# RWKV-7 delta rule on one core: u's products between y's products with the state, and the second half of the grams ahead of the rest of y

## What is computed

```
def step(S, inp):
    r_t, w_t, k_t, v_t, kk_t, b_t = inp
    sa = jnp.einsum('bhvk,bhk->bhv', S, kk_t)
    S = S * w_t[:, :, None, :] - sa[..., None] * b_t[:, :, None, :] + v_t[..., None] * k_t[:, :, None, :]
    return S, jnp.einsum('bhvk,bhk->bhv', S, r_t)
```

## Time and profile before

| | us |
|---|---|
| median of 3 runs | 1451.32 (1449.02 to 1452.41) |
| the profiled execution | 1445.32, of which the span is 1443.5 |
| PE busy | 1371.0 (95%) |
| PE weight loads | 1207.8 (84%) |
| DVE busy | 778.6 (54%) |
| ACT busy | 614.1 (43%) |
| POOL busy | 240.5 (17%) |

### The profile page before, as it was taken

How to read it: one execution, slowest core, us unless ns; L and a number is a source line. 1 busy time by engine, 2 the same in 40 slices (tenths; PEclk the granted TensorE clock), 3 DMA queues, 4 the chain that set the end, 5 groups by cost and what they waited for, 6 DMA issues and landing times. The chain is left out here.

```text
span 1443.5 us, 32955 instructions
## 1 busy us (share of the span) xinstructions
PE 1371.0 (95%) x13740; PEld 1207.8 (84%) x13740; DVE 778.6 (54%) x1588; ACT 614.1 (43%) x1230; POOL 240.5 (17%) x335
## 2 busy tenths in 40 slices
PE   7999999999999899999999899999999999998997
PEld 7989899887899788888888568899999997665885
DVE  6737344687750157788788543741111213875445
ACT  6725345777851123344334431531111133886224
POOL 0000000000000146677566400000001000213000
PEclk9999999999999979899899999999999999999999
DMA  5723323567778254556564363042324355230202
GB/s 211 222 67 70 98 78 104 142 169 214 220 202 227 64 101 104 116 125 148 133 135 105 96 240 133 1 175 85 90 90 110 90 145 189 87 118 23 89 30 94
DMA packets 265269, 178.43 MB, mean 124 GB/s; under 512 B 169599, under 2 KB 239167, under 8 KB 264207
## 3 DMA queue, kind: packets, MB, share of 16 engines
q1 hardware_dynamic: 233159, 161.37, 39.5%
q10 hardware_dynamic: 31968, 15.04, 3.6%
HBM read 116.21 MB, written 60.46 MB: 122 GB/s over the span
## 5 line engine op out<-in xcount | busy, mean ns | idle before, releaser
L369 PE MATMUL mix_acc<-mix_high,mix_w_high 128*128 128x364 f32 (+1 forms) x768 | 178.6, 341 | 12.4 <-ACT mix_high L435 10.0
L369 PE MATMUL mix_acc<-mix_low,mix_w_high 128*128 128x364 f32 (+1 forms) x768 | 172.2, 333 | 0.6 <-DVE mix_low L589 0.6
L369 PE MATMUL mix_acc<-mix_high,mix_w_low 128*128 128x364 f32 (+1 forms) x768 | 171.1, 332 | 0.0
L369 PEld LDWEIGHTS mix_acc<-mix_high,mix_w_high 128*128 128x128 f32 x768 | 130.4, 190 | 32.1 <-issue 28.4
L369 PEld LDWEIGHTS mix_acc<-mix_low,mix_w_high 128*128 128x128 f32 x768 | 133.4, 190 | 1.2 <-DVE mix_low L589 0.9
L369 PEld LDWEIGHTS mix_acc<-mix_high,mix_w_low 128*128 128x128 f32 x768 | 134.0, 190 | 0.0
L603 DVE TENSOR_TENSOR mix_w_low<-mix_wt,mix_w_high 128x1024 fp32r<-128x1024 f32 x32 | 39.2, 1224 | 127.6 <-ACT mix_w_high L441 127.3
L1612 PE MATMUL out_acc<-qkvg_room_r_high,qkvg_room_w_high 128*128 128x364 f32 (+1 forms) x320 | 105.8, 331 | 1.4 <-DVE qkvg_room_w_low L1964 1.4
L1612 PE MATMUL out_acc<-qkvg_room_r_low,qkvg_room_w_high 128*128 128x364 f32 (+1 forms) x320 | 105.1, 329 | 0.0
L1612 PE MATMUL out_acc<-qkvg_room_r_high,qkvg_room_w_low 128*128 128x364 f32 (+1 forms) x320 | 105.1, 328 | 0.0
L455 ACT ACTIVATE mix_out<-mix_acc 128x364 f32<-128x364 f32 (+1 forms) x96 | 38.3, 472 | 146.0 <-PE mix_acc L369 145.9
(11 more groups left out here) (282 smaller groups left out, 3130.3 us busy)
## 6 DMA issues: line engine op xcount, KB each, us to landing
mix_wt<-in_w_in SPq DMA_DIRECT2D x32, 512.0 KB, 4.6
qkvg_room_wt<-in_w_att SPq DMA_DIRECT2D x20, 512.0 KB, 3.7
delta_bk<-scr_bk SPq DMA_DIRECT2D x68, 128.0 KB, 3.4
delta_kr<-scr_kr SPq DMA_DIRECT2D x17, 512.0 KB, 6.6
scr_kr<-mix_outs SPq DMA_DIRECT2D x16, 512.0 KB, 4.0
scr_bk<-mix_outs SPq DMA_DIRECT2D x16, 512.0 KB, 4.7
early_xpad<-in_xpad SPq DMA_DIRECT2D x8, 548.5 KB, 8.7
scr_xg<-early_xs SPq DMA_DIRECT2D x8, 544.0 KB, 3.0
```

The lines of the kernel that those rows point to most:

```text
L369: mm = pe.matmul(acc[:, s, k, 0:width], w[:, s, d, :], r[:, d, n0:n0 + width], start=d == 0 and q == 0, stop=d == DT - 1 and q == 2)
```

## The change

`make_u` and `begin_y` become one function, `make_u_and_begin_y`. For each pair it issues u's two products with the result in the other half (`FLIPPED`), so in off-diagonal quarters, and then y's two products with the state, in diagonal ones. The wait for `normed` (the centring and scaling of the chunk before, which uses the bank `wide`) stands ahead of all of them now. `turn_y` comes after both, then `make_grams(front, 1)`, then `end_y`. ScalarE's copies of u read the other half (`src[FLIPPED[p]]`), and the one-piece copy of chunk 16 to `lower` becomes two copies of 64 partitions.

```
-                def make_u(c):
+                def make_u_and_begin_y(c):
+
                     if c < SAMPLE:
                         pe.wait_ge(grown_kept, 6 * c + 6)
                     else:
                         pe.wait_ge(solved_wide, c + 1)
                     pe.wait_ge(z_kept, c + 1)
+                    if c:
+                        pe.wait_ge(normed, NORM * c)
                     for pair in range(DT):
+                        columns = slice(64 * pair, 64 * pair + 64)
+                        for p, half in enumerate(HALVES):
+                            u = pe.matmul(chain_bank[FLIPPED[p], columns], inverse(c, 1)[half, pair, :], z[half, pair, :], start=True, stop=True)
+                        if pair == DT - 1:
+                            u.then_inc(u_made, 1)
                         for half in HALVES:
-                            mm = pe.matmul(chain_bank[half, 64 * pair:64 * pair + 64], inverse(c, 1)[half, pair, :], z[half, pair, :], start=True, stop=True)
-                    mm.then_inc(u_made, 1)
+                            if c < SAMPLE:
+                                y = pe.matmul(wide_bank[half, columns], kr[half, c % 4, 1, pair, :], state[half, c % 2, pair, :], start=pair == 0, stop=False, skip_group_check=True)
+                            else:
+                                y = pe.matmul(wide_bank[half, columns], own_turned[half, pair, 1, :], unit64[half, :], start=pair == 0, stop=False, skip_group_check=True)
+                    y.then_inc(y_begun, 1)
...
                     if live(behind):
-                        make_u(behind)
+                        make_u_and_begin_y(behind)
                     if live(i - 2):
                         turn_y(i - 2)
...
-                    if live(behind):
-                        begin_y(behind)
-                        end_y(behind)
                     if live(front):
                         make_grams(front, 1)
+                    if live(behind):
+                        end_y(behind)
...
                     for p, half in enumerate(HALVES):
-                        act.activation(uv[half, c % 3, :, p, :], src[half], ACT.Copy).then_inc(u_kept, 1)
+                        act.activation(uv[half, c % 3, :, p, :], src[FLIPPED[p]], ACT.Copy).then_inc(u_kept, 1)
                     if c == SAMPLE:
...
-                        act.activation(lower[:], src, ACT.Copy).then_inc(u_plain_kept, 1)
+                        for p, half in enumerate(HALVES):
+                            act.activation(lower[half], src[FLIPPED[p]], ACT.Copy).then_inc(u_plain_kept, 1)
```

More of the change, by code:

```diff
@@ L1206, in make_s @@
                     mm.then_inc(s_made, 1)
-                def begin_y(c):
-                    if c:
-                        pe.wait_ge(normed, NORM * c)
-                    for pair in range(DT):
-                        for half in HALVES:
-                            o = wide_bank[half, 64 * pair:64 * pair + 64]
-                            if c < SAMPLE:
-                                mm = pe.matmul(o, kr[half, c % 4, 1, pair, :], state[half, c % 2, pair, :], start=pair == 0, stop=False, skip_group_check=True)
-                            else:
-                                mm = pe.matmul(o, own_turned[half, pair, 1, :], unit64[half, :], start=pair == 0, stop=False, skip_group_check=True)
-                    mm.then_inc(y_begun, 1)
                 def end_y(c):
@@ L1416, in _ @@
                         for b in range(NB):
-                            act.wait_ge(u_plain_kept, 1)
+                            act.wait_ge(u_plain_kept, 2)
                             act.activation(u_own[:, b], lower[:], ACT.Copy, scale=seq_mask[:, b:b + 1]).then_inc(u_owned, 1)
```

## The result

The changed kernel takes 1429.68 us (median of 4 runs, 1422.90 to 1432.47) against 1450.17 of the kernel before, now the median of four runs too: 20.5 us less, ratio 0.9854 with the 95% interval 0.9812 to 0.9896. The profiled execution took 1431.17 with a span of 1429.4, so 14.1 less than the span before. I had forecast 13.4 less and 1438, with 1429 as the lower end. The 95% interval of the first set stands for 15 to 27 us less, that of the second for 12 to 25: the size is known to some 6 us either way.

A forecast was written before the change was run, and what follows sets the result against it. PE and DVE are nearly full, bound by a ring of waits on PE's second grams. 15 turns x 0.93 = 14.0 us less, 0.6 back: 1445.3 to 1431.9 profiled, plus 6.0 gives 1438, range 1429 to 1446.

The forecast's parts named there:

- the ring of waits: DVE's second masks, block sums, GpSimd's pick, PE's spread, DVE's solve columns, y's scaling; waits each turn for PE's second grams.
- the turn: A middle turn at full clock goes from 16.83 us to some 15.9, 0.93 less, in turns 1 to 15.
- The block in four quarters: On PE, u and the begun y as 64 records take 1.03 us instead of 2.38; upper bound 2.22.
- The new wait and the DVE idle: PE waits some 0.74 us before second grams; DVE's 0.95 before second masks goes; reciprocal waits about 0.45.
- the loss at the third level products: On PE, the third level products wait for the inverse ready at 760.30, which costs 0.06 us.
- Turn 17: At the end of u's chain, ScalarE's copy of the second half adds 0.6 us.
- I expect as many falls as before: The clock falls to half level as often as before, give or take one or two, 4.4 us a fall.
- PE idled before the spread: Before the clock falls at 599 and 705, PE ran narrow second-level products, then idled ahead of the spread.
- The 6.0 carried over from the profile to the median: The median without a profile lies 6.0 us above the profiled execution; added again for the changed kernel, giving 1437.9.
- Rival B: The quarters of u and y do not overlap: block 2.22 us, turn gains about 0.55, time 1444.6; chance 0.12.
- Rival D: Slower: PE's moved idle makes the clock fall in more turns, 4.4 us each, 1460 with five more; chance 0.09.

The follow-up runs named there:

- e3: Changed kernel with u's products in the diagonal quarters, shared with y, order and alternation kept: 1429.2 us against 1446.7 before, ratio 0.9898.
- f1: The changed kernel as it is, run again beside more runs of the kernel before: 1428.8 us against 1449.1, ratio 0.9871.
- e4: Changed kernel with one extra 256-column matmul per turn, result overwritten, in PE's gap before the spread: 1430.5 us against 1446.7 before, ratio 0.9885.
- e1: Kernel before with only the order changed, second half of the grams ahead of the end of y: 1425.2 us against 1446.7, ratio 0.9867.
- e2: Changed kernel with the second grams back behind the end of y, four quarters kept: 1450.1 us against 1446.7 before, ratio 1.0031.
- g1: e2 with one extra 256-column matmul per turn where PE waits for ScalarE's copies of u: 1462.9 us against 1446.5 before, ratio 1.0112.

## Why the prediction was right or wrong

The direction was right, and so was the ring of waits. The size was not: 20.5 against 13.4. Two terms failed: the turn, taken at 0.93 where 1.05 was measured, and the clock, whose part in the difference I put at nothing and in the level at a fixed 6.0. By the prediction's steps:

- **The block in four quarters: right.** 1.10 for the 1.03 taken; without the quarters 2.02 for the 2.22 (e3). By the Trainium skill's rule ("TensorE: Matmul & The Clock Gate", "The mechanism") that weight loads overlap only across row groups, the four quarters would have taken what the diagonal took. The traces disagree with it, 1.10 us in the changed kernel against 2.02 in e3.
- **The new wait and the DVE idle: right.** 0.70 for 0.74; the second masks' wait is gone; the reciprocal waits 0.52 for the 0.45 forecast.
- **The turn: too small, 0.93 for 1.05.** I took the idle of 0.95 as the gain. But a DVE instruction starts about 0.07 before the end printed for the one ahead of it (742.86 against 742.28 + 0.65), so from start to start the removed wait was worth 1.02: 753.45 - 751.85 = 1.60 before, 742.86 - 742.28 = 0.58 now. And I let the loss at the third level products stand (0.06), which did not come. 15 turns make 15.8 for 14.0: 1.8 us of the miss of 7.
- **Turn 17: right.** +0.6.
- **"I expect as many falls as before", and the clock left out of the difference: the larger part of the miss.** 15.8 less 0.6 makes 15.2. At 60 us of half clock the two lines lie 15 us apart, at 80 us 17 (16 to 18 by resampling the executions). So the layout of the turn accounts for the change at the same clock to within 2 us; this excess stays open. Most of the other 3 us of the 20.4 in f1's set is how long the clock happened to be down in the executions compared: 77 us for 84 in the kernel before, 2.5 us at 0.385 each. The first set can't be split that way, since of its kernel before only the profile has a clock on record.
- **The number of falls was right, their length not.** From the begun z of turn 1 to that of turn 15, 14 turns, the profile of the kernel before has 249.1 us, which is 13.3 more than 14 x 16.84. The two profiles of the changed kernel have 232.2 and 230.8, so 11.1 and 9.7 more than 14 x 15.79. Each has two falls after the stretch at 550. In the kernel before both last 10 us and cost 4.3 to 4.4 in their turn; in the changed kernel one lasts 10 us and costs 4.0 to 4.1, the other lasts 3.4 and costs 0.9. That is the 2 to 4 us, in three single profiles.
- **"PE idled before the spread" ahead of the falls at 599 and 705: wrong for the first.** PE had stopped 0.89 without a releaser ahead of the level products, and did not wait before the spread (the rows under e4).
- **The 6.0 carried over from the profile to the median: wrong.** It is no property of the kernel. The profiled execution of the kernel before, 1445.3 at a clock of 0.976, was one of its less disturbed; that of the changed kernel, 1431.2 at 0.971, lies 3.0 above the median of its three others. For the profiled execution I had 1431.9, and 1431.2 came: a hit that is partly luck, for its 14.1 are 16.0 gained from the first grams of turn 1 to those of turn 15 (248.78 and 232.78), 4.3 lost ahead of them, where the granted clock from 500 to 560 was 0.66 for 0.80, and 2.4 gained behind.
- **Rival B, too low in its price.** I had PE bind the turn at 0.55 gained if nothing overlaps. The most common turns gained 1.01 in e3 and 0.87 in e1, the mean ones 0.80 and 0.64. The step that failed is the block at its upper bound with a further idle for its start: the second grams start 3.69 after the first in e3 where I had 3.90, and the level products 0.4 earlier than before where I had 0.2, enough for the block sums to stay the latest in a turn in which PE does not stop.
- **Rival D was real, in another kernel.** e2 has the shorter turn and no gain, g1 is 16 us slower. In the changed kernel the gap before the spread got shorter instead (0.67 for 1.02).

What the title of the change names first, the overlap of u and y, is worth 0.04 of the 1.05 by e3's most common turn (the quarters alone) and 0.18 by e1's (with the alternation). By the means of the turns and at the same clock it is worth more, 4 to 7 us of the 17, which fits the slack that it leaves PE for its stops; in the median times nothing of this is seen, since e1 and e3 spent less time at half clock. Alone (e2), the quarters gained nothing in time. The order of the grams is the larger part by every measure.

## What to carry to other kernels

Look for the ring of waits across engines and move the producer that the ring waits for; here two lines of order did what the overlapped products could not, because their time came out of a wait. Where single executions scatter by a per cent, plot each one's time against its time at half clock: here that turned a scatter of 17 us from lowest to highest into one of 1.4 about a line, and told a change of the work from a change of the clock. Read all turns at full clock and not only the most common one, for a rare stop of an engine lengthens the turn only where that engine has no slack. A shorter turn can lose all its gain to the clock, as in e2, if it leaves PE idle beside sparse products.

## What was not expected of the hardware

- One matmul of 0.6 to 0.7 us per turn that computes nothing, in a gap of 1.0 to 1.2 behind narrow products, took 14 us off (1435.2 against 1449.1); from 560 to 790 the granted clock of the profiled execution was 1.00 for 0.96.
- A product of 64x64 float32 in two diagonal quarters runs at about 32 ns a record (2.02 for 64), in four at 17 (1.10 for 64).
- The falls can lock on to the turn: in g1 every turn from 694 on had one, and each took 20.47 us.
- A microsecond at half clock costs the whole program 0.385 us in the kernel before (38 executions) and 0.28 in the changed one (10).
- PE stops for 0.4 to 1.2 us with nothing in the profile that it waits for, in some turns and not in others (0.39 at 741.25 before, 0.85 at 664.11 after); several long falls of the clock follow such a stop.
